# A streaming encoder step on one core: initial loads chained, norm weights moved to GpSimd, one B1 projection ahead of B2

## The reference

```
for each layer:
  h = RMSNorm(x) * g_norm           # 1024 channels
  P = h @ w_in                      # q, k, v, gates of four branches
  A: index scores, top-k of the keys (bitwise threshold search), attention over the chosen keys
  B: forgetting attention: logits get F[t] - F[s], F = cumsum(log sigmoid(.))
  C: attention in a band of 9 chunks of 64 tokens, with a learned bias
  M: cross attention into 256 memory rows: RMSNorm(mem) * g_mem @ w_mem_kv
  x = x + concat(branches * silu(gates)) @ w_out
y = RMSNorm(x) * g_final
```

## Time and profile before

| | us |
|---|---|
| three runs | 1706.81, 1709.91, 1711.33 (median 1709.91) |
| profiled execution | 1708.8 |
| its span | 1707.0 |
| TensorE busy | 1683.4 (99%) |
| VectorE busy | 1012.5 (59%) |
| ScalarE busy | 656.3 (38%) |
| GpSimd busy | 241.7 (14%) |

### The profile page before, as it was taken

How to read it: one execution, slowest core, us unless ns; L and a number is a source line. 1 busy time by engine, 2 the same in 40 slices (tenths; PEclk the granted TensorE clock), 3 DMA queues, 4 the chain that set the end, 5 groups by cost and what they waited for, 6 DMA issues and landing times.

```text
span 1707.0 us, 30025 instructions
## 1 busy us (share of the span) xinstructions
PE 1683.4 (99%) x10773; PEld 1094.6 (64%) x10773; DVE 1012.5 (59%) x2707; ACT 656.3 (38%) x1586; POOL 241.7 (14%) x452
## 2 busy tenths in 40 slices
PE   8999999999999999999999999999999999999998
PEld 4466677767778755555444777767677786555553
DVE  4745888878878233333235378887888772333321
ACT  3532334333343345454124323343333433445531
POOL 1233321100010000002022433210000001000000
PEclk9999999999999999999999999999999999999999
DMA  9444322222132323114431533241231324220130
GB/s 316 177 141 126 127 94 89 95 78 106 41 135 93 103 80 102 37 44 119 127 106 50 176 103 123 90 140 41 81 109 38 132 97 128 63 90 38 45 109 37
DMA packets 66722, 171.88 MB, mean 101 GB/s; under 512 B 11456, under 2 KB 36000, under 8 KB 64144
## 3 DMA queue, kind: packets, MB, share of 16 engines
q1 hardware_dynamic: 49968, 131.14, 23.7%
q0 software_dynamic: 16608, 38.83, 6.9%
HBM read 142.29 MB, written 30.73 MB: 101 GB/s over the span
## 4 chain that ended last, share of the span: by engine, by line
PE 77%; DVE 15%; DMA 2%; issue 2%; ACT 2%; DVEq 1%; ACTq 1%; SPq 0%
PE psX L933 52%; DVE lower L1333 8%; PE psT L859 7%; PE psX L1109 6%; PE psS L1042 6%; DVE work L1564 2%; PE psS L961 2%; DMA wring<-in_w 1%; PE psX L859 1%; PE psX L1084 1%; DMA hT<-in_xT 1%; ACT gate L1150 0%; DMA scratch_xres<-xr 0%; PE psS L859 0%; DVE sc L1429 0%
## 5 line engine op out<-in xcount | busy, mean ns | idle before, releaser
L933 PE MATMUL psX<-wring,hT 128*128 128x512 f32 (+2 forms) x2016 | 835.5, 558 | 6.9 <-DMA wring<-in_w 3.8
L933 PEld LDWEIGHTS psX<-wring,hT 128*128 128x128 f32 x2016 | 364.7, 190 | 329.9 <-issue 321.0
L1333 DVE TENSOR_SCALAR_CACHE_REDUCE lower<-sc,thr 128x640 uint8<-128x640 f32 (+5 forms) x462 | 407.3, 933 | 17.6 <-issue 9.5
L933 PE MATMUL psX<-hT,wring 128*128 128x128 f32 x2880 | 334.6, 275 | 0.6 <-ACT gate L1223 0.3
L933 PEld LDWEIGHTS psX<-hT,wring 128*128 128x128 f32 x2880 | 327.7, 192 | 3.3 <-issue 2.6
L1265 ACT ACTIVATE work<-work,stat 128x256 f32<-128x256 f32 (+7 forms) x288 | 200.0, 695 | 293.1 <-DVEq L1567 290.5
L1274 ACT COPY work<-psT 128x512 f32<-128x512 f32 (+2 forms) x352 | 156.8, 488 | 322.4 <-PE psT L859 321.0
L859 PEld LDWEIGHTS psT<-con,work 128*128 128x128 f32 x1080 | 121.4, 141 | 73.2 <-issue 66.9
L859 PE MATMUL psT<-con,work 128*128 128x128 f32 x1080 | 158.2, 278 | 0.0
L1564 DVE CUSTOM_DVE_ANT_0 work<-psS,bias 128x640 f32<-128x640 f32 (+7 forms) x120 | 86.2, 718 | 40.8 <-PE psT L859 20.0
L1564 DVE CUSTOM_DVE_ANT_0 work<-psS,sc 128x384 f32<-128x384 f32 (+5 forms) x48 | 42.7, 890 | 72.5 <-PE psT L859 70.7
(11 more groups left out here) (207 smaller groups left out, 1515.2 us busy)
## 6 DMA issues: line engine op xcount, KB each, us to landing
wring<-in_w SPq DMA_DIRECT2D x17, 2048.0 KB, 9.5
cache<-in_kB SPq DMA_DIRECT2D x16, 512.0 KB, 5.9
cache<-in_vB SPq DMA_DIRECT2D x16, 512.0 KB, 4.0
cache<-in_kC SPq DMA_DIRECT2D x16, 512.0 KB, 6.2
cache<-in_vC SPq DMA_DIRECT2D x16, 512.0 KB, 4.3
scratch_oscr<-gate POOLq DMA_DIRECT2D x54, 128.0 KB, 2.0
hT<-scratch_oscr SPq DMA_DIRECT2D x18, 384.0 KB, 3.7
kv<-in_x SPq DMA_DIRECT2D x9, 512.0 KB, 9.9
```

The costliest lines, as they stand in the source:

```text
L933: mm = pe.matmul(out, lhs, rhs, start=(kt == 0), stop=(kt == KT - 1))
L1333: v.tensor_scalar(lower[:, at:at + STRIP_L[t]], sc[:, o], thr[:, n:n + 1], 0.0, ALU.is_lt, ALU.add, accum_out=below[:, n:n + 1])
```

## The change

1. On SP, the second head of A1's weights is issued when turned tile 0 has landed, the third when the first head has landed, and turned tile 1 (with all that is queued behind) when the second head has landed.
2. The weighing of tiles 0, 1, 2 stays with VectorE; from tile 3 on, and for the memory tiles in both layers, GpSimd does it. The memory tiles' weighing becomes a step of its own, emitted right before their `norm`, and their `turn` on VectorE waits for it. Its place in the order is the same as VectorE's was for tiles 3 to 8: behind `turn n-1` of iteration n for tile n+2.
3. B1 of tile 0 is projected before B2 of the samples. In the main loop B2 ST_ takes its place; `iw 2` and the rounds follow the first unit of the loop as before.

```diff
@@ program_order
                 if n in (5, 6):
+                    emit("weigh", n + 4)
                     emit("norm", n + 4)
...
             elif n in (2, 3):
+                emit("weigh", NT + n - 1)
                 emit("norm", NT + n - 1)
...
-        emit("Pp", "B2", ST_, 0, 3)
+        emit("Pp", "B1", 0, 0, 3)
         emit("is", 2)
-        emit("Pp", "B2", ST_, 3, 6)
+        emit("Pp", "B1", 0, 3, 6)
         emit("is", 3)
-        emit("P", "B2", ST_)
+        emit("P", "B1", 0)
         emit("Q", ("B", "s0", 0, 1))
-        units = [(c, t) for pair in (("B1", "B2"), ("C1", "C2")) for t in [ST_] + TILES[:NT] for c in pair][2:]
+        units = [(c, t) for pair in (("B1", "B2"), ("C1", "C2")) for t in [ST_] + TILES[:NT] for c in pair]
+        units = [u for u in units if u not in (("B1", ST_), ("B1", 0))]
...
-            if (c, t) == ("B1", 0):
+            if (c, t) == ("B2", ST_):
                 emit("iw", 2)
...
@@ SP
+                    if s[1] == "x1":
+                        sp.wait_ge(s_head[1], 16)
...
+                    if s[1] == 1:
+                        sp.wait_ge(*xT_loaded["x0"].on("x0"))
+                    elif s[1] == 2:
+                        sp.wait_ge(s_head[0], 16)
                     cols = slice(s[1] * D, (s[1] + 1) * D)
                     sp.dma_start(wring[:, 0, cols], d["w"][0:P, cols]).then_inc(s_head[s[1]], 16)
@@ VectorE
-                if k == "weigh":
+                if k == "weigh" and by_dve(l, s[1]):        # l == 0 and n < 3
...
                     if comes_turned(l, n):
-                        if n > ST_:
-                            weigh(l, n)
...
+                        if n > ST_:
+                            dve.wait_ge(*w_pool.on(n))
@@ GpSimd
+                if k == "weigh" and not by_dve(l, s[1]):
+                    n = s[1]
+                    weights, loaded = weights_of(l, n)
+                    pool.wait_ge(*loaded)
+                    g.tensor_tensor(turned_tile(n), turned_tile(n), weights, ALU.mult).then_inc(w_pool.sem, 1)
```

More of the change, by code:

```diff
@@ L331, in program_order @@
                 spare[0] = 0.0
-                pace[0] = sum(cost(x) for x in rounds) / (units.index(("M1", 5)) - units.index(("B1", 0)) - 1)
+                pace[0] = sum(cost(x) for x in rounds) / (units.index(("M1", 5)) - 1)
             settle()
@@ L627, in encoder @@
         small_loaded = Signal(sem("small_loaded"), [(l, "g") for l in range(DEPTH)], lambda e: 16)
-        weighed = Signal(sem("tile_weighed"), events(["weigh"], lambda s: s[1]))
+        by_dve = lambda l, n: l == 0 and n < 3
+        w_dve = Signal(sem("tile_weighed_by_dve"), [(l, s[1]) for l, s in steps("weigh") if by_dve(l, s[1])])
+        w_pool = Signal(sem("tile_weighed_by_pool"), [(l, s[1]) for l, s in steps("weigh") if not by_dve(l, s[1])])
         xT_loaded = {x: Signal(sem(f"turned_{x}_loaded"), [(l, x) for l in range(DEPTH) if not l or x == "m"], lambda e: 16)
@@ L727, in turned_tile, with weights_of @@
             return hT[:, first:, n * P:(n + 1) * P]
+        def weights_of(l, n):
+            x = [x for x in TURNED_IN if n in TURNED_IN[x]][0]
+            c0 = C_GT + KT * (l + 1 if n > ST_ else 0)
+            return con[:, c0:c0 + KT].unsqueeze(2).to_broadcast([P, KT, P]), xT_loaded[x].on(x)
         def tile_of(l, n):
@@ L899, in _ @@
                             elif l == 0:
-                                pe.wait_ge(*weighed.on(t))
+                                pe.wait_ge(*(w_dve if by_dve(l, t) else w_pool).on(t))
                             else:
@@ L1319, in rotate @@
                 return v.tensor_tensor(x2, x2, u1, ALU.add)
[L1321 to L1327, removed]
             def count_below(strips_):
@@ L1339, in _ @@
                 k = s[0]
-                if k == "weigh":
-                    if s[1] == 0:
+                if k == "weigh" and by_dve(l, s[1]):
+                    n = s[1]
+                    if n == 0:
                         dve.wait_ge(s_ident, 16)
-                    weigh(l, s[1]).then_inc(weighed.sem, 1)
+                    weights, loaded = weights_of(l, n)
+                    dve.wait_ge(*loaded)
+                    v.tensor_tensor(turned_tile(n), turned_tile(n), weights, ALU.mult).then_inc(w_dve.sem, 1)
                 elif k == "norm":
@@ L1704, in out_rows @@
                     return rows(d["p" + name], l, SEQ, t * P, P)
-                if k == "P" and s[1][0] == "O":
+                if k == "weigh" and not by_dve(l, s[1]):
+                    n = s[1]
+                    weights, loaded = weights_of(l, n)
+                    pool.wait_ge(*loaded)
+                    g.tensor_tensor(turned_tile(n), turned_tile(n), weights, ALU.mult).then_inc(w_pool.sem, 1)
+                elif k == "P" and s[1][0] == "O":
                     c, t = s[1:]
```

## The result

The changed kernel took 1722.12 us (median of 6 runs, 1719.81 to 1723.48), the kernel before 1709.53 us beside it (6 runs): a ratio of 1.0077, with an interval of 1.0066 to 1.0088. It is slower, by 12.6 us, where 1708.4 had been predicted and no more than 1713.5 allowed for. The profiled execution has a span of 1721.7 us, 14.7 more than before. Of the five runs of edit 3 alone one took 1934.14 us at a mean granted clock of 0.849, and is left out of the comparisons.

A forecast was written before the change was run, and what follows sets the result against it. TensorE was taken as the bound, busy 1683.4 of 1707.0 us. The profiled 1708.8 - 1.75 (projection order) + 0.2 (loads) + 0 (GpSimd weighing) gave 1707.2; with the median 1.1 higher, 1708.4 us was predicted, range 1703.5 to 1713.5.

The forecast's parts named there:

- Edit 3, "I take 0": Weighing by GpSimd from tile 3: VectorE loses 12.3 us of work, TensorE gains 0, with 5.2 us as bound.
- The duration itself: GpSimd's 128x1024 weighing: about 2.3 us, bounded by 1.23 us from below and 2.9 us from above.
- Rival C: At tiles 5 and 6, GpSimd's arithmetic is held by its own DMA issues: 1718.2 us; chance 0.08.
- Edit 1, taken as +0.2: Initial loads on SP: tile 2 lands when the stream has brought the same bytes, plus pauses; a loss of 0.2 us.
- pauses of a few tenths: Initial load stream: pauses of a few tenths, with most of 512 KB still under way at each wait.
- the bounds of -1.75 to +5.8: Initial loads: best, x2 landed at 16.7, a gain of 1.75 us; worst, at 24.6, a loss of 5.8 us.
- the sign that I had named for being wrong (after 24): Start of A1: unit 0 turned before 20 or after 24 would show the forecast wrong.
- Edit 2, taken as -1.75: B1 of tile 0 before B2: covers the weights waits of 1.25 and 0.50 us, minus 1.75 us.
- What is late next: nothing near: After B1 goes before B2: B1 weights and tile 0 are there, top-k rounds begin at the same unit and pace.
- the two waits behind the memory tiles' turns stayed: TensorE's two waits behind the turned memory tiles remain, at 1.5 to 2 us.
- rival A: VectorE's relief also removes turn waits (3.6) and relu waits (1.6): 1703.0 us, 1701.2 with best loads; chance 0.09.

The follow-up runs named there:

- edit 3 alone: The kernel before with only GpSimd's weighing from tile 3 and of the memory tiles: 1720.35 us, ratio 1.0063; 1718.99 us in a second, single run.
- without edit 3: The kernel before with the chained initial loads and B1 ahead of B2, all weighings on VectorE: 1713.28 us, ratio 1.0023.
- the kernel with three tiles back: The changed kernel with the weighing of tiles 6, 7 and memory tile 9 back on VectorE: 1718.84 us, ratio 1.0058.
- the eight pieces: The changed kernel with each of GpSimd's ten weighings cut into eight tensor_tensor of 128x128: 1715.37 us, ratio 1.0031.
- tiles 3 and 4 alone: The changed kernel with GpSimd weighing only tiles 3 and 4 of layer 0, the other eight on VectorE: 1714.33 us, ratio 1.0026.
- one-input kernel: The changed kernel with GpSimd weighing a tile by eight tensor_scalar of 128x128 instead of one tensor_tensor: 1719.71 us, ratio 1.0064.
- the wait before tile 1 alone: The kernel before with only turned tile 1 waiting for the second head, heads issued at once: 1711.16 us, ratio 1.0012.
- the loads alone: The kernel before with only the three waits on SP that chain the initial loads: 1710.74 us, ratio 1.0013.
- the swap alone: The kernel before with only B1 of tile 0 projected ahead of B2 of the samples: 1709.15 us, ratio 0.9997.
- the first four experiments: Not numbered in the text; listed first are loads, GpSimd's weighing and swap, each alone, then loads with swap: ratios 1.0013, 1.0063, 0.9997, 1.0023.

## Why the prediction was wrong, point by point

**Edit 3, "I take 0": the step that failed.** The sum priced GpSimd's instructions (will the tile be ready?) and what VectorE gives up, but not what GpSimd's work does to VectorE's other work. With the sixteen undisturbed tensor_tensor of the earlier trace rows I argued from a stretch in which no score step was near, and said so, and still took 0. The term measured 9.2 us (ratio 1.0077 against 1.0023 without edit 3). The traces show an instruction of VectorE standing still for the length of two weighings, 0.88 us becoming 4.52 at 66.81 of the kernel with three tiles back. That this is the cause is shown by the eight pieces (the stall goes, 6.8 us back) and by tiles 3 and 4 alone (no loss). The Trainium skill's rule ("GPSIMD Engine Reference", 8. Key points) names the pair of engines, and two kinds of VectorE instruction: those with two SBUF inputs, and those in a 2-port perf mode. I applied it to the one whose time I had just estimated, GpSimd, and not to the one that TensorE waits for, and I left out the second kind. The TENSOR_SCALAR of 68.45 has one tile as input and a factor per partition, and was held as well (4.66 for 0.55 us). It may be of that second kind: undisturbed it takes 0.42 us at 384 columns and 0.55 at 640, 0.5 ns a column, where the score step with two inputs takes 0.62 and 0.88, 1.0 ns a column. No run tells it from another cause.

The duration itself was well sized: 1.91 us, where 2.3 had been estimated, and the bounds held.

**Rival C** had the size (1718.2) but in the changed kernel not the mechanism: TensorE never waited for GpSimd there. The weighing of tile 5 began at 47.25, behind the issue of 46.71 that had stood for 7.32 us, as before, and ended at 49.16, about 1 us before its use. Only the one-input kernel, with 5.47 us for a tile, went late at that place.

**Edit 1, taken as +0.2:** the path was right, the size off. As foretold the first matmul came earlier (at 7.63, 6.6 foretold), tile 2 was issued at 12.09 in place of 9.60, and tile 2's landing set the turn of unit 0. The term that failed is "pauses of a few tenths": the stream paused for longer, with 210 to 218 GB/s at a DMA share of 0.66 to 0.81 between 6 and 10.5 us, and again behind 15.

```profile
7.50:9.00 1.50, 1.37 (x4) 0.68 (x4) 0.00 (x0) 0.00 (x0) 0.00 (x0) 1.00 0.66 218
...
15.00:16.50 1.50, 0.64 (x2) 0.00 (x0) 0.27 (x1) 0.00 (x0) 0.00 (x0) 1.00 0.57 195
```

It isn't one pause in particular: with the wait before tile 1 alone the stream runs at 295 to 393 GB/s from 6 to 10.5 us and drops to 186 and 112 at 10.5 and 15, and tile 2 is as late. The loss was 1.9 us in the trace with the loads alone and 2.9 with all three edits, 2.2 by the ratio, within the bounds of -1.75 to +5.8. The turn of unit 0 at 24.55 was also the sign that I had named for being wrong (after 24).

**Edit 2, taken as -1.75:** both waits for weights went, as said, and the time did not (-0.5 us by the ratio of the swap alone). "What is late next: nothing near" was wrong: a copy on ScalarE behind VectorE's search rounds, some 54 us behind the wait that was saved. Here too VectorE held the limit; the saving of TensorE's wait ended at the next place that VectorE sets.

**Right:** the two waits behind the memory tiles' turns stayed (1.64 and 2.04 us), and rival A with them is refuted; relief of VectorE by 12.3 us brought nothing that any row shows. In the changed kernel it was no relief, since VectorE was busy 1.7 us longer and not 12 less; but with the eight pieces, where VectorE is hardly held, the two waits are still there, 1.83 and 2.04 us.

**What stays open.** Why the first step of 54.84 was held through GpSimd's three DMA issues too (57.26 to 58.94), and that of 53.04 with edit 3 alone likewise, while in the kernel with three tiles back a step beside such issues alone, at 65.80, took its usual 0.88 us: no run tells. Nor does any tell what decides which engine goes first. Nor was it tried what the swap brings where the search rounds are paced otherwise.

## What to carry to other kernels

Before work goes from one elementwise engine to another, lay the new instruction beside each instruction of the first engine that will run at the same time, and price that one as standing still for the whole length of the new one, and of the next if two follow each other. If it must be moved, cut it into short pieces and put it where the first engine has no work that a bound engine waits for. A wait saved on the bound engine is worth only what the next place, set by another engine, leaves of it: look for the next small wait (here 0.26 us) and ask who sets it.

## What the runs showed of the hardware that was not expected

- A 128x1024 float32 tensor_tensor in place with a broadcast factor takes GpSimd 1.91 us and VectorE 1.226, 1.56 times as long. In eight pieces it takes GpSimd 2.89 us, as eight one-input tensor_scalar 4.7 to 7.0 us.
- VectorE held beside a weighing of GpSimd: 0.20 to 1.51 us (128x48, two inputs), 0.75 to 4.33 (128x512, two inputs), 0.88 to 4.52 (128x640, two inputs), 0.55 to 4.66 (128x640, one tile). Its 128x1024 product with PSUM as second input (1.22 us) ran beside GpSimd's weighing of 47.25 unstretched.
- A wait of 2 us on TensorE may bring half clock or not. Behind the wait of 1.97 to 1.98 us in the last units of A1 the clock stayed at 1.00 before and with the swap alone, and with the wait before tile 1 alone, and fell to 0.50 in the four kernels with all of edit 1's loads and no weighing of GpSimd beyond tile 4. With more on GpSimd the wait is 2.04 us, and the clock fell behind it with edit 3 alone and stayed at 1.00 in the changed kernel. Over the runs of the kernel before beside the first four experiments, eleven with a mean clock of 0.999 have spans of 1705.5 to 1707.3 us, thirteen with 0.998 spans of 1705.9 to 1709.5, two with 0.997 spans of 1709.7 and 1711.1: part of the spread between runs of one kernel goes with the clock. That a change which moves waits moves it too is not shown.
